# Every second residual sum behind the four output norms taken by GpSimd, with signals of its own

## The reference, cut to what matters

```
def rmsnorm(x, g):
    y = xf * lax.rsqrt(jnp.mean(xf * xf, axis=-1, keepdims=True) + EPS)
    return y.astype(x.dtype) * g

for i in range(2):                       # layers 2 and 3 of the kernel
    h = modulate_2(rmsnorm(x, g_pre_mix[i]), shift_m, scale_m)
    y = attention(h) @ w_o   if i == 0 else   multiscale_pool_mix(h)
    x = x + gate_m * rmsnorm(y, g_post_mix[i])
    h = modulate_2(rmsnorm(x, g_pre_ffn[i]), shift_f, scale_f)
    x = x + gate_f * rmsnorm(conv_ffn_2(h, ...), g_post_ffn[i])
return x
```

## Time and profile before

| | |
|---|---|
| median of 3 runs | 1625.56 us (1623.44 to 1626.12) |
| the profiled execution | 1623.06 us |
| its span | 1620.9 us |
| mean granted TensorE clock | 0.986 |
| TensorE busy | 1553.9 us (96%) |
| VectorE busy | 1055.0 us (65%) |
| ScalarE busy | 839.4 us (52%) |
| GpSimd busy | 98.4 us (6%) |

### The profile page before, as it was taken

How to read it: one execution, slowest core, us unless ns; L and a number is a source line. 1 busy time by engine, 2 the same in 40 slices (tenths; PEclk the granted TensorE clock), 3 DMA queues, 4 the chain that set the end, 5 groups by cost and what they waited for, 6 DMA issues and landing times.

```text
span 1620.9 us, 27655 instructions
## 1 busy us (share of the span) xinstructions
PE 1553.9 (96%) x9546; PEld 1279.1 (79%) x9546; DVE 1055.0 (65%) x1819; ACT 839.4 (52%) x1517; POOL 98.4 (6%) x152
## 2 busy tenths in 40 slices
PE   5999989999999999799899999999999999899997
PEld 3777667688888888697789998797788887588886
DVE  4443874756665477666678876754668865778865
ACT  4442872544444223455656655536556654566653
POOL 0111000000000111020000000020100001000000
PEclk9999999999999999999999999999999999799999
DMA  9765105332322587342177558442866688636663
GB/s 371 284 217 190 40 1 212 113 104 91 101 93 84 188 275 244 109 141 87 44 262 261 184 182 318 146 152 83 338 223 188 179 276 293 243 116 183 180 186 115
DMA packets 77091, 287.52 MB, mean 177 GB/s; under 512 B 8993, under 2 KB 12577, under 8 KB 67025
## 3 DMA queue, kind: packets, MB, share of 16 engines
q1 hardware_dynamic: 61056, 190.23, 37.2%
q0 software_dynamic: 15952, 96.18, 15.8%
HBM read 282.44 MB, written 1.05 MB: 175 GB/s over the span
## 4 chain that ended last, share of the span: by engine, by line
PE 81%; DVE 10%; issue 3%; ACT 3%; DMA 2%; DVEq 1%; SPq 0%; ACTq 0%
PE B L1810 15%; PE B L1811 15%; PE B L1812 15%; PE B L1827 11%; PE B L1825 6%; PE B L1847 3%; DVE WLO L1152 3%; PE B L2091 2%; PE B L1839 1%; PE B L1841 1%; PE B L1840 1%; PE B L2145 1%; PE B L1994 1%; DVE Y L1591 1%; PE B L2013 1%
## 5 line engine op out<-in xcount | busy, mean ns | idle before, releaser
L1152 DVE TENSOR_TENSOR WLO<-RAW,WHI 128x1024 fp32r<-128x1024 f32 (+1 forms) x376 | 412.1, 1099 | 168.7 <-ACT WHI L701 163.9
L701 ACT ACTIVATE WHI<-RAW 128x1024 fp32r<-128x1024 f32 (+1 forms) x376 | 358.4, 958 | 161.8 <-PE B L1812 90.7
L1810 PE MATMUL B<-HHL,WHI 128*128 128x256 f32 (+1 forms) x1168 | 395.7, 339 | 10.0 <-DVE HHL L1260 7.3
L1812 PE MATMUL B<-HHL,WLO 128*128 128x256 f32 (+1 forms) x1168 | 389.3, 333 | 0.0
L1811 PE MATMUL B<-HHL,WHI 128*128 128x256 f32 (+1 forms) x1168 | 389.2, 333 | 0.0
L1810 PEld LDWEIGHTS B<-HHL,WHI 128*128 128x128 f32 x1168 | 222.5, 190 | 48.8 <-issue 18.3
L1827 PE MATMUL B<-HHL,WHI 128*128 128x512 f32 x704 | 244.0, 399 | 3.6 <-DVE WLO L1152 1.9
L1812 PEld LDWEIGHTS B<-HHL,WLO 128*128 128x128 f32 x1168 | 222.6, 191 | 21.6
L1811 PEld LDWEIGHTS B<-HHL,WHI 128*128 128x128 f32 x1168 | 222.7, 191 | 20.2
L1825 PE MATMUL B<-HHL,WLO 128*128 128x256 f32 x704 | 184.0, 281 | 0.0
L1827 PE MATMUL B<-MID,WHI 128*128 128x512 f32 x462 | 162.6, 400 | 0.1
(11 more groups left out here) (237 smaller groups left out, 2170.5 us busy)
## 6 DMA issues: line engine op xcount, KB each, us to landing
RAW<-in_wup SPq DMA_DIRECT2D x176, 512.0 KB, 3.7
GWR<-in_wmod POOLq DMA_DIRECT2D x33, 1024.0 KB, 8.6
RAW<-in_wdn SPq DMA_DIRECT2D x64, 384.0 KB, 3.5
RAW<-in_wproj SPq DMA_DIRECT2D x44, 512.0 KB, 4.6
RAW<-in_wdn SPq DMA_DIRECT2D x64, 320.0 KB, 3.6
GWA<-in_wmod POOLq DMA_DIRECT2D x19, 1024.0 KB, 6.3
WINV<-in_wmod POOLq DMA_DIRECT2D x32, 512.0 KB, 5.6
RAW<-in_wout SPq DMA_DIRECT2D x24, 512.0 KB, 3.7
```

The lines of the kernel that those rows point to most:

```text
L701: act_f(WH[s][:, 0:kts, :], RAW[s][:, 0:kts, :], ACT.Copy).then_inc(hi_done, 1)
L1152: v.tensor_tensor(WL[s][:, 0:kts, :], RAW[s][:, 0:kts, :], WH[s][:, 0:kts, :].bitcast(F32), ALU.subtract).then_inc(lo_done, 1)
L1810: mm(bank[:, 0:t], wh, a, start=first and k == ks[0], stop=False)
L1812: ins = mm(bank[:, 0:t], wl, a, start=False, stop=stop and k == ks[-1])
```

## The change

GpSimd gets a function `add_back(key, c)` and takes the sums of chunks 0 and 2 of all four norms; VectorE keeps those of chunks 1 and 3. The semaphore `resid` becomes two: `resid[0]` counts GpSimd's sums, `resid[1]` VectorE's, each by one, and whoever waited for `resid` waits for the one of its chunk. VectorE's order becomes post 0, post 1, add 1, post 2, post 3, add 3. GpSimd's sums stand in its list at written-out places: both of (2, "p1") between units (9,1) and (9,2); those of (2, "p2") before and behind unit (11,1); those of layer 3 at the end.

```diff
-        nt_ready, nh_ready, nl_ready, resid = sem("nt_ready"), sem("nh_ready"), sem("nl_ready"), sem("resid")
+        nt_ready, nh_ready, nl_ready = sem("nt_ready"), sem("nh_ready"), sem("nl_ready")
+
+        resid = [sem("resid_g"), sem("resid_v")]
...
-                sp.wait_ge(resid, 8 * 3 + 2 * c + 2)
+                sp.wait_ge(resid[c % 2], 2 * 3 + c // 2 + 1)
...
+            def add_back(key, c):
+
+
+                gp.wait_ge(post_t, 4 * POST[key] + c + 1)
+                x = X[:, 2 * c:2 * c + 2, 0:256]
+                gp.tensor_tensor(x, x, NORM[256][:, 0:2, :], ALU.add).then_inc(resid[0], 1)
...
                 unit(9, kt)
+                if kt == 1:
+                    for c in (0, 2):
+                        add_back((2, "p1"), c)
...
             unit(11, 0)
             tables(3)
-            for kt in range(1, 8):
+            add_back((2, "p2"), 0)
+            unit(11, 1)
+            add_back((2, "p2"), 2)
+            for kt in range(2, 8):
                 unit(11, kt)
+            for c in (0, 2):
+                add_back((3, "p1"), c)
+            for c in (0, 2):
+                add_back((3, "p2"), c)
...
-                act.wait_ge(resid, 8 * (POST[l - 1, "p2"] if which == "n1" else POST[l, "p1"]) + 2 * c + 2)
+                act.wait_ge(resid[c % 2], 2 * (POST[l - 1, "p2"] if which == "n1" else POST[l, "p1"]) + c // 2 + 1)
...
                     def post(c):
                         if c >= 2:
-                            dve.wait_ge(resid, base + 2 * c - 2)
+                            dve.wait_ge(resid[c % 2], 2 * POST[key] + c // 2)
...
-                    post(0)
-                    for c in range(1, 4):
+                    for c in range(4):
                         post(c)
-                        add_back(c - 1)
-                    add_back(3)
+                        if c % 2:
+                            dve.wait_ge(post_t, base // 2 + c + 1)
+                            x = X[:, 2 * c:2 * c + 2, 0:256]
+                            v.tensor_tensor(x, x, NORM[256][:, 2:4, :], ALU.add).then_inc(resid[1], 1)
```

## The result

The changed kernel takes 1627.32 us in the median (1622.62 to 1638.70, 19 runs), the kernel before 1622.10 in the same comparison (1619.02 to 1626.12, 19 runs). The ratio is 1.0032, 95% interval 1.0019 to 1.0045: slower by 5.2 us. The forecast was +0.65 us, which counted as "same", with 0.70 for same and 0.22 for slower beyond 0.2%. The measured median lies in the stated range, but what happened was the less likely case: slower by more than 0.2%.

A forecast was written before the change was run, and what follows sets the result against it. By the chain that ended last, 81% TensorE and 10% VectorE; norm steps count only where TensorE or the end waits. Terms +1.1 + 0 - 0.4 - 0.05 = +0.65 us, median forecast 1626.2 us, range 1623.0 to 1630.2.

The forecast's parts named there:

- The end, -0.05 us: At (3, "p2"), the last norm: the last sum ends 0.05 us earlier and the four stores follow as before.
- both slower ones: Two rivals: late units with cold clock (+4.55 us, chance 0.15) and GpSimd's sum waiting for post (+4.35 us, chance 0.12).
- The range: Stated for the median: 1623.0 us, to take in true overlap, up to 1630.2, to take in both slower rivals.
- A GpSimd sum, 1.25 us: In all four norms: a GpSimd addition of 128x512 takes 1.25 us, bounds 0.61 to 1.5.
- The two engines block each other: In the norms: VectorE's sums and GpSimd's, both reading SBUF, block whoever starts second; VectorE's last 1.2 to 1.3 us, not 0.68.
- true overlap: Rival, in the norms: GpSimd's addition takes 1.04 us without blocking VectorE; -2.2 us, 1623.4, chance 0.18.
- GpSimd's sum also waits for post: Rival, in the norms: posts 1 and 3 block GpSimd's sums, sum 3 ends at +6.2; +4.35 us, 1629.9, chance 0.12.
- The order inside a norm, +5.08 for the last sum: Inside a norm: the last sum ends 5.08 us after post 0 starts, against the old +5.13; nothing gained.
- (2, "p1"), the transfers, +1.1 us: At (2, "p1"): units (9,2), (9,3) issued 4.6 and 3.0 us later; the landing TensorE awaits comes +1.1 us, bounds 0 to +3.0.
- Late units and a cold clock: Rival, at (2, "p1"): the units' delay goes through in full and TensorE's clock halves; +4.55 us, 1630.1, chance 0.15.
- (2, "p2"), 0: At (2, "p2"): the square of chunk 2 waits for TensorE, not the sum, and transfers stay covered; 0 us.
- (3, "p1"), -0.4: At (3, "p1"): ScalarE's squares of chunk 2, and TensorE's last column sums with them, start earlier; -0.4 us.

The follow-up runs named there:

- b1: The kernel before, plus one idle GpSimd memset behind the last post, which nobody waits for: 1626.80 us, ratio 1.0020 to the kernel before.
- b2: The kernel before, with only chunks 0 and 2 of the last norm (3, "p2") summed by GpSimd: 1627.39 us, ratio 1.0021.
- b3: The kernel before, with only chunk 0 of the last norm summed by GpSimd, VectorE summing 1, 2 and 3: 1624.65 us, ratio 1.0014.
- b4: The kernel before, plus one idle GpSimd memset placed six weight blocks before the last one: 1623.02 us, ratio 0.9991.
- e3: e2, with VectorE's posts 1 and 3 of the first three norms written to a free PSUM bank and summed from there: 1622.04 us, ratio 0.9996.
- e1: The changed kernel, with all four sums of the last norm VectorE's again: 1621.44 us, ratio 0.9984; timed again, 1621.54 us, ratio 0.9996.
- b0: The kernel before, unchanged, timed against itself as if it were another kernel: 1621.02 us, ratio 0.9991.
- e2: e1, with units (9,2) and (9,3) issued where they had been in the kernel before: 1622.18 us, ratio 0.9984.

## Why the prediction was right or wrong

*The end, -0.05 us: wrong, and the failed step.* The term was "The four stores follow as before". They do, and the sums end 0.02 us earlier (1618.05 against 1618.07). But I took the landing of the last store for the end of the kernel. What showed in its place: the drain of GpSimd, which ends 7.7 to 7.8 us behind its last instruction, ends last, and SyncE waits 4.6 us longer at the barrier. b1, b2, b3 and b4 show a tail of this length behind GpSimd's last instruction, an addition or a memset, wherever it stands. None of my rivals had it: both slower ones put their price at (2, "p1") or into a post that blocks, and the change came out near theirs (+4.55 and +4.35 against +5.2) for another reason. Two rows of the trace of before would have raised the question: the drain at line 155, 16.0 us long, and GpSimd's last instruction at 1385.8; the price behind an addition they do not give. I asked what covers GpSimd's transfers, never what covers the close of its program.

*The range: kept by luck.* I laid the change on the median of three runs, 1625.56. The 19 runs of the kernel before in the comparison have 1622.10. On that median the same range, -2.6 to +4.6 us, would end at 1626.7, below the measured 1627.32. The forecast of 1626.2 is near only because the kernel before was 3.5 us faster than I had taken it to be, which made up for most of the missing drain.

*A GpSimd sum, 1.25 us: right.* 1.26 to 1.28 us in all eight. The estimate by the rule of the Trainium skill, GPSIMD Engine Reference, section 3.1 Elementwise, was 1.30; both hold within 0.04.

*The two engines block each other: right, and with it the rival "true overlap" has fallen.* VectorE's sums took 1.08 to 1.28 us, and e3 shows the cause by taking the second SBUF operand away: 0.69. Post, with one operand in PSUM, ran through beside GpSimd; the rival "GpSimd's sum also waits for post" has fallen (GpSimd's sum began 0.09 us after post 0, under post 1). The sentence of the Trainium skill, SBUF — State Buffer, Who interferes with whom, which spares an instruction with at most one SBUF input, agrees with the trace here: 0.69 us beside GpSimd.

*The order inside a norm, +5.08 for the last sum: right*, 5.1 at (2, "p1") and 5.07 at (3, "p2").

*(2, "p1"), the transfers, +1.1 us: mechanism there, size too large.* Unit (9,3) was issued 5.1 us after post 0 (forecast 5.1, before 2.1). It landed 15.3 us after it in the changed kernel, 15.05 in e1, against 14.8 in before and 14.3 in b0: 0.3 to 1.0 us late in single profiles, and TensorE began the up-projection 0.3 to 0.7 us late in e1. The gap in GpSimd's queue was there: from 5 to 7 us after post 0 it moved 0.48 MB in the changed kernel and 0.85 in before, which at 0.42 MB per us is a gap of 0.9 us (forecast 0.65). The landing was late by no more than about that, so the further share that I gave to the weight blocks was too much. That the delay goes through to TensorE in full failed in the changed kernel, where TensorE reached the unit 1.3 us after its landing. In the time nothing of it is seen: e1 and e2 are equal. "Late units and a cold clock" has fallen as a mechanism: the cold clock is there, in kernels with the old order too.

*(2, "p2"), 0: right.* The square of chunk 2 began 5.49 us after post 0, before 5.50, both times for TensorE's sake.

*(3, "p1"), -0.4: right in one profile, of no use in others.* In the changed kernel this stage is 0.6 us shorter than in before. But in the eight traces with 12.5 us, among them e1 with GpSimd's sums and b0 without, TensorE's column sums run at half clock from the start (eight take 1.87 us, in before 1.05) and set the end by themselves, and the sums of X, however early, are covered.

## What to carry to other kernels

Before work is moved to an engine that had finished early, look at how the program closes on it: every engine's drain stands in the trace, and the kernel ends with the last. Here GpSimd must be done about 7.8 us before the last store lands, or its drain is the end; a single memset past that point costs nearly as much as real work. And a stage difference of one or two microseconds in a single pair of profiles, where TensorE's clock moves, is tested against a second profile of the unchanged kernel before it is given a cause.

## What the runs showed of the hardware that was not expected

GpSimd's closing drain ended 7.7 to 7.8 us behind the end of its last memset or addition (six kernels with additions, two with a memset). It took 16.0 us in both traces of before, where GpSimd's last instruction was the issue of a 1 MB transfer; the transfer landed 12.1 us after its issue, so the drain ended 3.9 us behind the landing. What it waits for was not tested. The other engines' drains at the same place took 0.01 to 1.3 us. The Trainium skill, VectorE: DVE Perf Modes, section The DRAIN you can't avoid, gives about 12 ns for the drains of preamble and postamble, on all five engines. SyncE's 7 to 13 ns at line 155 agree with this figure and GpSimd's do not; whether the drains of line 155 are of the kind that the page means, no trace here shows.

The addition brought a MODIFY_POOL_CONFIG into GpSimd's stream at 1158.8 us, and the first sum began at 1160.67, 0.09 us after its post had ended. No cost of it was seen here.
